# Experts packed by rank in grains of 32 rows, and weights held back until the first gather has landed

## The chip, the cores and the metric

The kernel runs on one core of one Trainium2 chip, in float32 throughout, as one launch. The metric is device time in microseconds (us); the median of three runs before is 3216.39 us.

## What is computed

A trunk of two layers over 1024 image tokens and 256 context tokens of width 1024. A layer is adaptive modulation, attention (differential attention over all tokens in layer 1, windowed attention with sinks in layer 2), a residual, and a hierarchical mixture of experts. Layer 1 sends 1280 tokens through the experts, layer 2 only the 1024 image tokens. The part that matters here, with `h` the normed tokens:

```python
grp    = argmax(softmax(h @ w_r1 + b_r1))              # one of 4 groups
p_in   = softmax((h @ w_r2 + b_r2)[grp])               # 8 experts of the group
top_p, top_j = top_k(p_in, 2);  top_p /= sum(top_p)
expert = grp * 8 + top_j                               # 2 of 32 experts a token
y      = (silu(g) * u) @ w2[expert],  g, u = split(h @ w13[expert])
out    = sum over the two experts of p_grp * top_p * y
```

`w13` of an expert is 1024 x 1024 and `w2` is 512 x 1024 (4 MiB and 2 MiB). Which rows belong to which expert is known only at run time.

## The kernel before

Every layer has five stages with a barrier of all engines between them (`phase_end`): front (modulation, QKV), attention, post (output projection, residual, norm, router logits), route (tables of where each row goes), and the experts. After layer 2 a last stage adds the weighted expert outputs. In the text, layer 1 is `l = 0` and layer 2 is `l = 1`.

*Post* (lines 1220 to 1357). One step for each tile of 128 tokens: PE makes the output projection (L1265), DVE takes it (L1307, L1308), DVE scales it (L1317), POOL shifts it (L1356), PE turns it (L1246), ACT and DVE copy it (L1334, L1288), PE makes the logits of the tile before (L1254) and DVE adds their bias (L1293).

*Route* (`dve_route`, L1401). DVE picks for all tiles together the group and the two experts of each token as one-hot rows, counts rows of each expert before each tile (L1439), PE adds them up over the partitions (L1553 to L1555), and DVE works out how many blocks of 128 and halves of 64 rows each expert needs. It writes `exptab`, the expert of each block, which SP reads to load weights (L1467), then for each row a block and a lane; 16 or 20 small pairs of one-hot maps (L1511, L1512) go through PE (L1559) and give `toktab` and `rowtab`, the token that is gathered for each lane of each block and the row that is scattered to (L1517 to L1521).

*Experts* (L1631 to L1942). The work is a fixed list of units of 128 rows. A unit is either one expert's block ("B") or two halves of 64 rows for two experts ("P"), by the strings `ORDER`: 27 units in layer 1, 23 in layer 2, 35 blocks or halves of each layer with 3 weight pieces of 2 MiB each: two for `w13`, one for `w2`. Pieces go one after another through a ring of nine slots: SP waits until the piece nine before has been used (L1615) and issues a transfer (L1616). The first nine are issued in the route stage as soon as `exptab` is there (L1634), before the barrier. POOL clears the gather buffers (L1642), loads a few constants in layer 1 (L1646), and gathers the tokens of a unit by an indirect DMA (L1655) up to two units ahead; it scatters a unit's output (L1662). PE does for unit i: gate/up (L1707, 16 products of 128 x 128 by 512, or 32 with 64 columns, whose two halves write to different PSUM partitions), turning the tokens of unit i+1 (L1691), down of unit i-1 (L1728), turning h of unit i (L1739). In the trace each float32 product is two records, one a pass. ACT and DVE copy in between. Rows that find no room go to fallback blocks (L1863 to L1942): a loop that runs at least once, each trip loading three pieces (L1857, L1859) and working one block of 128 rows with nothing overlapped.

## Time and profile before

| what | before |
|---|---|
| median of 3 runs | 3216.39 us (3216.09 to 3216.54) |
| profiled execution, its own time | 3216.31 us |
| its span, first to last instruction | 3214.7 us |
| PE busy | 2896.9 us (90%) |
| DVE, ACT, POOL busy | 40%, 25%, 21% |
| mean granted TensorE clock | 0.951 |
| read from and written to memory | 662.32 MB, 87.62 MB |
| first expert stage, first to last unit | about 1223 to 1827 us |
| second expert stage, first to last unit | about 2594 to 3122 us |

The span is the profiled execution from its first to its last instruction; times in the rows are microseconds from its start. A busy share is the part of a stretch in which the engine had an instruction; idle time counts only where the engine is what the end waits for. The granted clock is a share of 2.4 GHz.

### The profile page before, as it was taken

Reading aid. Unit: us, or ns where it says so; the run is one execution under the profiler, and the core shown is the slowest. Engines: PE = TensorE matmul, PEld = TensorE weight load, DVE = VectorE, ACT = ScalarE, POOL = GpSimd, SP = SyncE. Lnnn points to the kernel's source line nnn. Section 1 sums busy time; section 2 is a strip of 40 time slices with the busy share of each in tenths; the row PEclk is TensorE's granted clock in tenths of the full one; section 3 lists DMA queues with packets and bytes.
Section 4 is the critical chain, followed back from the end, with each engine's and each line's share of the span. In section 5 each row is a group of like instructions: output and inputs, shape, how many; then the busy total and the mean of one; then the engine's idle time right before and its main releaser. Section 6 shows DMA issues by size and latency. Waiting matters only on the chain. (4 is left out here: it accounts for less than half of the span.)

```text
span 3214.7 us, 34383 instructions
## 1 busy us (share of the span) xinstructions
PE 2896.9 (90%) x13041; PEld 1615.1 (50%) x13041; DVE 1299.6 (40%) x2274; ACT 792.7 (25%) x1763; POOL 689.5 (21%) x931
## 2 busy tenths in 40 slices
PE   7999998999999947999999959979999579999993
PEld 3444335888884533444444424468875334443431
DVE  4544204898882252111111154469972521111114
ACT  2211102777771100000000043146641000000001
POOL 2555201555452110010000024510001110000001
PEclk9999999999999958999999979989999789999996
DMA  6334576242413248999999574343322399999995
GB/s 252 100 102 138 199 267 176 52 98 50 99 54 128 92 188 332 412 386 415 383 413 389 216 270 135 88 124 56 67 67 93 130 410 427 426 427 427 426 417 208
DMA packets 205154, 734.36 MB, mean 228 GB/s; under 512 B 29376, under 2 KB 124784, under 8 KB 168896
## 3 DMA queue, kind: packets, MB, share of 16 engines
q1 hardware_dynamic: 104800, 633.33, 52.7%
q10 hardware_dynamic: 84896, 61.07, 5.8%
q0 software_dynamic: 15296, 37.78, 3.0%
q8 instruction: 104, 1.70, 0.2%
q14 instruction: 58, 0.48, 0.1%
HBM read 662.32 MB, written 87.62 MB: 233 GB/s over the span
## 5 line engine op out<-in xcount | busy, mean ns | idle before, releaser
L1707 PE MATMUL psum<-moe_ring,moe_xT 128*64 128x512 f32 (+1 forms) x2240 | 707.9, 602 | 15.6 <-DMA moe_ring<-in_e_w 13.3
L407 PE MATMUL psum<-qkv_w,act_hT 128*128 128x512 f32 x1376 | 612.0, 598 | 1.4 <-ACT act_hT L508 1.3
L1707 PEld LDWEIGHTS psum<-moe_ring,moe_xT 128*64 128x64 f32 (+1 forms) x2240 | 277.3, 162 | 410.4 <-issue 408.4
L407 PEld LDWEIGHTS psum<-qkv_w,act_hT 128*128 128x128 f32 x1376 | 256.6, 192 | 309.2 <-issue 306.9
L1728 PE MATMUL psum<-moe_ring,moe_hT 128*64 128x512 f32 (+1 forms) x1120 | 352.8, 594 | 1.6 <-DVE moe_hT L1808 1.6
L1804 DVE TENSOR_TENSOR moe_hh<-psum,moe_sg 128x512 f32<-128x512 f32 x50 | 34.6, 692 | 668.4 <-PE psum L1707 668.4
L1265 PE MATMUL psum<-wo,out_oT 128*128 128x512 f32 x576 | 255.6, 599 | 1.4 <-DVEq L1281 1.0
L1728 PEld LDWEIGHTS psum<-moe_ring,moe_hT 128*64 128x64 f32 (+1 forms) x1120 | 133.1, 160 | 184.6 <-issue 180.4
L1013 DVE TENSOR_REDUCE att_nmax<-psum 128x1 f32<-128x1280 f32 (+1 forms) x160 | 204.2, 1276 | 29.0 <-PE psum L906 28.0
L906 PE MATMUL psum<-att_kT,att_q 128*128 128x512 f32 (+1 forms) x832 | 198.0, 370 | 10.0 <-ACTq L137 5.1
L969 ACT ACTIVATE att_prob<-psum,att_nmax 128x1280 f32<-128x1280 f32 (+1 forms) x160 | 185.3, 1158 | 56.4 <-DVE att_nmax L1013 53.0
L1655 POOL DMA_INDIRECT moe_xg<-h_d,toktab x52 | 52.9, 1018 | 681.9 <-PE psum L1691 674.4
L1772 ACT ACTIVATE moe_sg<-psum 128x512 f32<-128x512 f32 x50 | 29.9, 598 | 670.9 <-PE psum L1707 670.9
L887 POOL TENSOR_SCALAR att_epsum<-att_den 128x1 f32<-128x1 f32 x80 | 112.7, 1408 | 325.9 <-DVE att_coef L1019 325.9
L954 PE MATMUL psum<-act_V,att_aT 128*128 128x128 f32 x1344 | 167.9, 279 | 4.1 <-DVE att_aT L1040 4.1
L1265 PEld LDWEIGHTS psum<-wo,out_oT 128*128 128x128 f32 x576 | 107.9, 192 | 126.7 <-issue 124.8
L906 PEld LDWEIGHTS psum<-att_kT,att_q 128*128 128x128 f32 x832 | 146.2, 191 | 38.2 <-ACT att_prob L969 6.1
L954 PEld LDWEIGHTS psum<-act_V,att_aT 128*128 128x128 f32 x1344 | 156.2, 192 | 9.8 <-DVE att_aT L1040 7.7
L605 POOL TENSOR_TENSOR qkv_t<-qkv_xn,qkv_rope 128x128 f32<-128x128 f32 (+1 forms) x264 | 133.0, 534 | 53.5 <-DVE qkv_xn L715 53.5
L1662 POOL DMA_INDIRECT y_d<-moe_yo,rowtab x50 | 50.3, 1005 | 395.3 <-ACT moe_yo L1778 395.3
L1068 PE MATMUL psum<-att_k,att_q 128*128 128x256 f32 x704 | 124.7, 305 | 6.9 <-ACTq L137 4.7
L911 PE MATMUL psum<-cst,att_prob 128*128 128x128 f32 x672 | 99.7, 277 | 18.8 <-DVE att_prob L1022 10.9
(252 smaller groups left out, 3301.7 us busy)
## 6 DMA issues: line engine op xcount, KB each, us to landing
moe_ring<-in_e_w SPq DMA_DIRECT2D x216, 2048.0 KB, 16.2
ada_w<-in_ada_w SPq DMA_DIRECT2D x48, 1024.0 KB, 6.5
qk_d<-qkv_stg ACTq DMA_DIRECT2D x112, 256.0 KB, 2.8
att_q<-qk_d SPq DMA_DIRECT2D x32, 640.0 KB, 12.5
att_q<-qk_d SPq DMA_DIRECT2D x64, 256.0 KB, 5.1
qkv_w<-in_a_wqkv SPq DMA_DIRECT2D x6, 2048.0 KB, 9.4
att_kT<-qk_d SPq DMA_DIRECT2D x32, 320.0 KB, 5.7
prep_y<-y_d SPq DMA_DIRECT2D x10, 1024.0 KB, 7.3
```

Of the source, the lines that this page charges most:

```text
L407: ins = nc.tensor.matmul(psum[:, u.par, :], hT[:, k, u.t * P:(u.t + 1) * P], qw[:, u.C % 2, k], start=(k == 0), stop=(k == KD - 1))
L605: ins = nc.gpsimd.tensor_tensor(dst[:, :, a, b, :], src[:, :, a, 1 - b, :], sn, ALU.mult)
L887: ins = nc.gpsimd.tensor_scalar(epsum[:, q], den[:, q, 0:1], den[:, q, 0:1], EPS, ALU.mult, ALU.mult)
L906: ins = nc.tensor.matmul(psum[:, 3 * m + b, 0:hi - lo], aq0[buf][:, m, x, t * P:(t + 1) * P], kT[buf][:, m, lo:hi], start=x == 0, stop=x == 1)
L911: ins = nc.tensor.transpose(psum[:, bank, (b - lo) * P:(b - lo + 1) * P], prob0[:, 2 * (n % 2), b * P:(b + 1) * P], ident)
L954: ins = nc.tensor.matmul(psum[:, 7, 0:P], aT0[:, n % 2, b, :], v, start=(b == 0), stop=(b == nb - 1))
L969: nc.scalar.activation(prob0[:, 2 * (n % 2) + m, 0:width], psum[:, 3 * m:3 * m + 3, :].rearrange("p b n -> p (b n)")[:, 0:width], ACT.Exp, ...
L1013: nc.vector.reduce_max(nmax[:, n % 2, m:m + 1], psum[:, 3 * m:3 * m + 3, :].rearrange("p b n -> p (b n)")[:, 0:width], AX, negate=True).th ...
L1068: ins = nc.tensor.matmul(o, aq1[:, half, m, j % 4, x, :], k, start=x == 0, stop=x == 1 and masked is None)
L1265: ins = nc.tensor.matmul(psum[:, 2 * par + n, :], oT[:, k, t * P:(t + 1) * P], wo[:, k, n * HALF:(n + 1) * HALF], start=(k == 0), stop=(k ...
L1707: ins = nc.tensor.matmul(psum[part, bank, :], xT[:, 4 * half + k, part], ring[:, w13[x, half] % RING, k, bank * DE:(bank + 1) * DE], start ...
L1728: ins = nc.tensor.matmul(psum[part, 5 + h, :], hT2[:, k, part], ring[:, w2[x] % RING, k, h * HALF:(h + 1) * HALF], start=(k == 0), stop=(k ...
```

## The change

The blocks and halves are replaced by grains of 32 rows. The 32 experts are ranked by their number of rows at run time, and each rank has a fixed room in grains (`ROOM`). The ranks are laid one after another, in the order that the string `STREAM` gives by room sizes, so that an expert may begin or end within a unit and a piece may serve two or more units. One rank of room 4 is left out of the units and takes the first fallback block (`own`), so 31 experts or 93 pieces stream through the ring. Within a unit all products have the same width: the largest of 1, 2 or 4 grains that divides each start and size (`columns`).

```diff
-ORDER = [("BBPBBPB" * 4)[1:], ("BP" * 12)[1:]]
+ROOM = [[5] * 3 + [4] * 5 + [3] * 12 + [2] * 11 + [1], [8, 8, 6, 5, 4] + [3] * 5 + [2] * 10 + [1] * 12]
+STREAM = ["4323532243235322432353224323312", "1218121822315213321312263122111"]
+GRAIN = 32
...
+        def columns(i):
+            width = max(n for n in (1, 2, 4) if all(at % n == 0 and size % n == 0 for r, at, size in UNITS[l][i]))
+            for r, at, size in UNITS[l][i]:
+                for b in range(at, at + size, width):
+                    yield r, slice(GRAIN * b, GRAIN * (b + width))
...
-                        for x in range(parts):
-                            part = slice(x * rows, (x + 1) * rows)
-                            ins = nc.tensor.matmul(psum[part, bank, :], xT[:, 4 * half + k, part], ring[:, w13[x, half] % RING, k, bank * DE:(bank + 1) * DE],
+                        for r, part in columns(i):
+                            ins = nc.tensor.matmul(psum[part, bank, :], xT[:, 4 * half + k, part], ring[:, CHUNK[l][r, half] % RING, k, bank * DE:(bank + 1) * DE],
```

A unit has one, two or four products of each kind side by side. A ring slot is given back when the last unit that uses its piece is done with it (`FREED`), and `s_used` counts half steps instead of pieces.

The first four pieces are issued in the route stage; the others wait until the first gather of tokens has landed:

```diff
+    HEAD = 4
...
     def sp_moe_first(sp, l):
         sp.wait_ge(s_exptab, l + 1)
-        sp_moe_loads(sp, l, 0, RING)
+        sp_moe_loads(sp, l, 0, HEAD)
 
     def sp_moe(sp, l):
-        sp_moe_loads(sp, l, RING, 10 ** 6)
+        sp.wait_ge(s_xg[0], xg_count(l, 0))
+        sp_moe_loads(sp, l, HEAD, 10 ** 6)
         sp_fallback(sp, l)
```

The picks are made tile by tile in the post stage, after the logits of the tile before (`dve_pick`, 19 DVE operations a tile, most of them chained):

```diff
+        def first_of(val, width, code, top, one):
+            low = lowfirst[:, NE - width:NE]
+            L(V_.reduce_max(top, val, AX))
+            L(V_.scalar_tensor_tensor(code, val, top, low, ALU.is_equal, ALU.mult))
+            L(V_.reduce_max(tops[:, 3:4], code, AX))
+            L(V_.tensor_scalar(one, code, tops[:, 3:4], None, ALU.is_equal))
...
             if later:
                 logit(t - 1, 1 - par)
+                dve.wait_ge(s_rld, 2 + T)
+                dvec.link(dve, dve_pick(dve, l, t - 1))
```

The route stage starts from the picks. It ranks the experts by count with a few small DVE steps and four small products on PE, writes `exptab` by rank, adds each rank's first row and room on PE, and makes the lane and block maps in two large operations for each of the two choices, in bf16, with the row number split over two sets of columns; 16 or 20 bf16 products of 154 columns replace the float32 ones of 80. POOL clears the gather buffers and loads the constants in the route stage (`pool_route`) instead of at the start of the experts:

```diff
+        V_.scalar_tensor_tensor(key[:, :], psum[:, 1, 0:NE], float(NE), iota[:, 0:NE], ALU.mult, ALU.subtract)
+        L(V_.scalar_tensor_tensor(keycol[small], psum[small, 3, 0:1], float(NE), col(0)[small], ALU.mult, ALU.subtract))
+        V_.tensor_scalar(ahead[small, 0], key[small], keycol[small], None, ALU.is_lt).then_inc(s_rtp, 1)
...
+        L(V_.tensor_copy(exptab[:, 0:NE], psum[:, 5, 0:NE]))
+        dve.sem_inc(s_exptab, 1)
...
+        for q in range(2):
+            V_.tensor_tensor(value[:, q, 0:nt, 1], onblk[:, q, 0:nt], cst[:, C_TOK:C_TOK + nt].unsqueeze(2).broadcast_to([P, nt, NBT]), ALU.mult)
+            V_.tensor_tensor(onlane[:, q, 0:nt], iota.unsqueeze(1).broadcast_to([P, nt, P]),
+                             lane[:, q, 0:nt].unsqueeze(2).broadcast_to([P, nt, P]), ALU.is_equal).then_inc(s_rtp, 1)
```

The shares of the two experts (`dve_shares`) are worked out at the start of the expert stage. The fallback loop runs once for `own` and once more for each block of rows beyond the rooms, and its gate/up waits for the two pieces of `w13` alone; `w2` has a semaphore of its own (`s_ow2`).

## Rows read from the trace of the kernel before

**Rows 1.** Stretches: us, busy time of each engine (records), PE clock, DMA share, GB/s.
```profile
1223.00:1827.00 604.00, 602.35 (x2004) 267.18 (x2004) 84.24 (x120) 48.78 (x82) 52.53 (x52) 0.99 0.94 380
2594.00:2858.00 264.00, 263.25 (x994) 110.51 (x996) 41.06 (x59) 21.61 (x36) 23.21 (x23) 0.99 1.00 421
2858.00:3104.00 246.00, 235.09 (x872) 98.69 (x871) 28.35 (x41) 17.93 (x30) 20.21 (x20) 0.98 1.01 427
```

**Rows 2.** Waits of PE from 2590 to 3170: us in total, times, longest.
```profile
PE psum L1707 <- DMA moe_ring<-in_e_w: 13.3, 6, 4.5
```

**Rows 3.** The chain that ended last: start us, us, what.
```profile
2580.38 11.09 DMA moe_xg<-h_d,toktab
...
3105.72 31.33 DMA moe_ring<-in_e_w
```

**Rows 4.** Timeline of PE in layer 1's experts: start us, us, what, records.
```profile
1242.32 13.95 PE L1707 MATMUL psum<-moe_ring,moe_xT 128*64 128x512 f32 x64
...
1264.54 13.90 PE L1707 MATMUL psum<-moe_ring,moe_xT 128*128 128x512 f32 x32
...
1286.86 13.47 PE L1707 MATMUL psum<-moe_ring,moe_xT 128*128 128x512 f32 x31
```

**Rows 5.** Timeline and durations (ns min/median/max) of the conditioning products, four side by side.
```profile
32.12 1.04 PE L374 MATMUL psum<-ada_w,ada_cs 128*2 128x512 f32 x8
...
L374 PEld LDWEIGHTS psum<-ada_w,ada_cs x384: 81/85/87, 11.6 to 523.6; 128*2 128x2 f32 x192
L374 PE MATMUL psum<-ada_w,ada_cs x384: 589/592/1061, 11.6 to 524.0; 128*2 128x512 f32 x192
...
L1707 PEld LDWEIGHTS psum<-moe_ring,moe_xT x2240: 132/137/337, 1223.6 to 3114.2; 128*64 128x64 f32 x100, 128*128 128x128 f32 x87
```

**Rows 6.** Timeline of DVE at the end of the post stages.
```profile
1137.22 1.23 DVE L1307 TENSOR_TENSOR postb_x<-psum,post_bc 128x1024 f32<-128x1024 f32 x1 [6.81 <-PE psum L1265]
...
1145.15 0.20 DVE L1293 TENSOR_TENSOR logits<-psum,brt 128x36 f32<-128x36 f32 x1 [1.92 <-PE psum L1254]
1147.71 0.69 DVE L1288 COPY postc_h2T<-psum 128x512 f32<-128x512 f32 x1 [2.37 <-PE psum L1246]
...
2535.45 0.20 DVE L1293 TENSOR_TENSOR logits<-psum,brt 128x36 f32<-128x36 f32 x1 [3.74 <-PE psum L1254]
```

**Rows 7.** Timeline of DVE and PE in layer 2's route stage.
```profile
2538.80 0.42 DVE L1410 TENSOR_TENSOR route_re<-route_re,route_ru 128x256 f32<-128x256 f32 x1
...
2545.65 1.54 DVE L1439 TENSOR_TENSOR route_pre<-route_pre,route_re 128x32 f32<-128x32 f32 x7
...
2551.93 0.95 DVE L1464 TENSOR_TENSOR route_cmp<-route_cum,cst 128x768 f32<-128x768 f32 x1
...
2554.27 0.18 DVE L1467 TENSOR_SCALAR exptab<-route_ebf 128x35 int32<-128x35 f32 x1
...
2569.24 7.12 PE L1559 MATMUL psum<-route_blk,route_lane 128*128 128x80 f32 x32 [19.19 <-DVEq L1514]
...
2577.41 0.20 DVE L1521 TENSOR_SCALAR toktab<-rowtab 128x80 int32<-128x80 int32 x1
```

**Rows 8.** Timeline of the start of layer 1's experts.
```profile
1209.28 1.14 POOL L1655 DMA_INDIRECT moe_xg<-h_d,toktab  x1 [5.96 <-DMA moe_xg<-in_consts]
...
1220.83 1.94 PE L1691 MATMUL psum<-cst,moe_xg 128*128 128x128 f32 x8 [21.81 <-DMA moe_xg<-h_d,toktab]
...
1223.68 2.05 PE L1707 MATMUL psum<-moe_ring,moe_xT 128*128 128x512 f32 x2 [0.91 <-issue]
```

**Rows 9.** Time to landing: the ring's first piece alone, then the two fallback gathers.
```profile
DMA to landing us min/median/max: 7.2/7.2/7.2
...
DMA to landing us min/median/max: 2.2/4.2/6.2
```

**Rows 10.** Queue of gathers and scatters (packets, MB, share); DMA over layer 2's experts (GB/s last).
```profile
q0 software_dynamic: 15296, 37.78, 3.0%
...
2611.00:3122.00 511.00, 497.36 (x1850) 209.81 (x1850) 61.66 (x90) 39.44 (x66) 42.43 (x42) 0.99 1.01 425
```

More of the change, by code:

```diff
@@ new lines, in build @@
+    mine = A("mine", [P, 2, TA, NE])
+    slot = A("slot", [P, 2, TA])
+    sloti = A("sloti", [P, 2, 2, TA], I32)
+    blkf = A("blkf", [P, 2, TA])
+    lane = A("lane", [P, 2, TA])
+    onlane = A("onlane", [P, 2, TA, P], BF16)
+    onblk = A("onblk", [P, 2, TA, NBT], BF16)
+    value = A("value", [P, 2, TA, 2, NBT], BF16)
+    table = A("table", [P, 2, NBT])
+    assert A.at <= M.at, (A.at, M.at)
+    key = R("key", [P, NE])
+    keycol = R("keycol", [P, 1])
+    ahead = R("ahead", [P, 2, NE])
@@ new lines, in pe_route @@
+        pe.wait_ge(s_rtp, 6 * l + 1)
+        nc.tensor.matmul(psum[small, 3, 0:2], tot[:, :], ones[:, 0:2], start=True, stop=True)
+        nc.tensor.matmul(psum[:, 1, 0:NE], ones[:, :], tot[:, :], start=True, stop=True).then_inc(s_rtm, 1)
+        nc.tensor.matmul(rank, tri, both[:, 0:nt], start=True, stop=False)
+        nc.tensor.matmul(rank, ones[:, :], pre[:, 0:nt], start=False, stop=False)
+        pe.wait_ge(s_rtp, 6 * l + 2)
+        nc.tensor.matmul(psum[:, 4, 0:NE], ones[small, :], ahead[small, 0], start=True, stop=True).then_inc(s_rtm, 1)
@@ L1603, in build @@
-    PLAN = chunk_plan()
+            for i in range(NU[l] + 1):
+                new = []
+                parts = {"half0": (i, 0), "up": (i, 1), "down": (i - 1, 2)}
+                for what, (n, piece) in parts.items():
+                    if not 0 <= n < NU[l]:
+                        continue
+                    for r, at, size in UNITS[l][n]:
+                        if (r, piece) not in chunk[l]:
+                            chunk[l][r, piece] = count
+                            new.append((count, r, piece))
+                            count += 1
+                        done[chunk[l][r, piece]] = (l, n, what)
+                    steps[1] += 1
+                    ready[l, n, what] = steps[1]
+                plan.append((l, i, new))
@@ L1605, in sp_moe_loads @@
+        return plan, chunk, ready, {n: ready[at] for n, at in done.items()}, count
+    PLAN, CHUNK, READY, FREED, _ = chunk_plan()
+    CHUNKS = [3 * (NE - 1) * (l + 1) for l in range(2)]
+    assert _ == CHUNKS[1]
     def sp_moe_loads(sp, l, first, last):
@@ L1742, in pe_moe @@
         turn_x(0)
[L1743 to L1745 removed]
+        for i in range(nu + 1):
             if i < nu:
[L1747 removed]
+                gate_up(i)
                 turn_x(i + 1)
             if i:
[L1750 removed]
+                down(i - 1)
             if i < nu:
@@ L1755, in used_by @@
     def used_by(l, i, what):
-        for pl, pi, w13, w2 in PLAN:
-            if pl == l and pi == (i if what == "up" else i + 1):
-                return 1 + max((w13 if what == "up" else w2).values())
+        return READY[l, i, what]
     def act_moe(act, l):
-        nu, base, xbase = len(UNITS[l]), UBASE[l], UBASE[l] + l
+        nu, base, xbase = NU[l], UBASE[l], UBASE[l] + l
         def take_x(i):
@@ L1840, in fallback_slot @@
     def fallback_slot(l, part):
-        return (sum(3 * (NBIG[n] + NSMALL[n]) for n in range(l + 1)) + part) % RING
+        return (CHUNKS[l] + part) % RING
     def sp_fallback(sp, l):
@@ L1846, in sp_fallback @@
         w2v = e_w2[l].rearrange("e (p k) f -> p e k f", p=P)
-        last = sum(3 * (NBIG[n] + NSMALL[n]) for n in range(l + 1)) + 2
         sp.wait_ge(s_fbtab, l + 1)
-        sp.wait_ge(s_used, last - RING + 1)
+        sp.wait_ge(s_used, max(FREED[CHUNKS[l] + part - RING] for part in range(3)))
         if l == 0:
@@ L1949, in build @@
     fu = A("u", [P, TX, D])
-    fxb = nc.alloc_sbuf_tensor_at("last_xb", [P, 5, D], F32, offset=arena0_at + 6 * 4 * D * 4)
+    SPARE = next(n for n in range(4, RING - 1) if not {n, n + 1} & {fallback_slot(1, part) for part in range(3)})
+    fxb = nc.alloc_sbuf_tensor_at("last_xb", [P, 5, D], F32, offset=arena0_at + SPARE * 4 * D * 4)
     def last_x(t):
```

486 lines of the change are left out of this document (236 added, 250 removed).

## The prediction, made blind

> **What bounds the kernel now.** I read four views in this order: busy time by stretch, PE's waits, one product of the expert stage followed in time, and the DMA's rate over the same stretch. The stretches show two expert stages of different kinds. In the first, from 1223 to 1827 us, PE is busy 602.35 of 604 us at a clock of 0.99, while the DMA engines have share 0.94 [rows 1]: PE alone is the bound. In the second the DMA share is 1.00 from 2594 and 1.01 from 2858 on, and PE falls to 235.09 busy of 246 us [rows 1]: there the weight stream is the bound. The waits agree: between 2590 and 3170 PE waits 13.3 us for weights, in six waits [rows 2]. At the end of that stage the chain waits 31.33 us, from 3105.72 to 3137.05, for the fallback block's weights [rows 3]. So a unit less is worth a whole unit in layer 1 (the first), and only its bytes in layer 2.
>
> **A unit in layer 1.** One unit is gate/up, turning the next tokens, down, and turning h. The unit with one expert starts at 1264.54 and the next at 1286.86: 22.32 us; the unit with two 64-row halves starts at 1242.32: 22.22 us [rows 4]. Two halves cost no more than one whole, since 64 records in 13.95 us stand against 32 in 13.90. I take 22.35 us. By the tables in the diff, layer 1 goes from 27 units to 23 and layer 2 from 23 to 19. In layer 1 that removes 4 x 22.35 = 89 us.
>
> **Is a set of four 32-column products as cheap as one?** By the plan 12 units of layer 1 and 11 of layer 2 run in width 32, with four products side by side. "Even widths" means that all products of a unit have its smallest common width. The nearest rows are the conditioning products, four at once with 2 columns each: 8 records (4 products, 2 passes) last 1.04 us, and one record alone 0.592 [rows 5]: with passes 0.434 us apart (13.90 us / 32 records [rows 4]) one product by itself would last 1.03. Their weight loads take 85 ns against 137 ns for 64 columns [rows 5], so 32 columns should take about 109 ns by the straight line. Four loads in a row are 0.44 us, just the length of a pass. Bounds of the extra cost of a four-part unit: below, 0 (a gain is excluded, since 512 columns stream either way); above, every load stands bare in front of its pass, 48 passes x 0.43 = 20.6 us. I take 0.15 us, because the two-part unit already shows loads of several tiles beside running passes for 0.05 us, and the four-way set of 2 columns shows it for four tiles. In sum 2 us in layer 1.
>
> The Trainium skill speaks against this: "TensorE: Matmul & The Clock Gate", section "Part 3: Packing small matmuls — row/col tiling", gives 3.07x for four tiles and 2.38x for three tiles of 32 columns, not 4x and 3x, and says that weight loads overlap running products only where the row group differs, which it doesn't here. By that a set costs 1.3 of one. Here the trace has two column tiles at 1.99x (13.95 against 13.90 us), which doesn't agree, and nothing with four full loads; the result that the rule gives is the second rival.
>
> **Fallback blocks.** I evaluated the reference's router on the reference's own inputs. Layer 1's experts need, in grains of 32 and by rank, 5 three times, 4 five times, 3 twelve times, 2 eleven times, 1 once: exactly the room given (94). Layer 2 needs 8, 8, 6, 5, then 3 six times, 2 ten times, 1 twelve times: all inside the room of 78. So no row overflows. Both kernels run one fallback block a layer; after, it holds the expert of rank 7 (rank 4 in layer 2). Its time, 24 us, is not changed. It waits for two of its three pieces instead of three.
>
> **Picks moved into the post stage.** 19 small DVE operations a tile. Seven linked ones take 1.54 us [rows 7], so 0.22 us each and 4.2 us a tile. They run between the logits of a tile and the next attention output, where DVE sits idle 6.81 us [rows 6]. So for all tiles but the last two they cost nothing; without that cover they'd cost up to 16 x 4.2 = 67 us. In the tail they are bare: the pick of the last but one tile starts at 1145.35 and ends near 1149.6, and pushes the copy at 1147.71 [rows 6] by 1.9 us; then come the last logits and a pick of 4.3 us. The same in layer 2: logits done 2535.65, now 2537.5, pick done 2541.9, barrier 2542.2.
>
> **Route stage, layer 2.** PE makes totals and ranks (3 us), then a ping-pong of small steps of 0.2 to 0.4 us with DVE for ranks of experts: the expert table is written some 4.2 us behind the barrier, at 2546.4, against 2554.45 now [rows 7]; the first weights go out 0.9 us later. PE's sums end at about 2548. Then DVE: 12 small steps 2.7, seven of 256 elements at about 0.4, 2.9, four small 0.8, two block maps of 616 elements 1.5, two values of 616 and two lane maps of 1024, 3.8 in all (0.95 us for 768 elements [rows 7]), 2559.8. 16 bf16 products follow, of which 8 lie behind the last map: 1.6 us against 7.12 now [rows 7]. Six steps for the table end at 2563, against 2577.6 now. Clearing the gather buffers (1.8 us) moves ahead, beside DVE's work. The gather goes out near 2563.9 instead of 2580.38 [rows 3]: 16.5 us earlier. In layer 1 the same steps with ten tiles give 1183.1 instead of 1209.28 [rows 8], 26 us earlier, since there the load of constants, now also ahead, had waited behind the ring's flood (about 6 us). Bounds of the new chain, some 50 dependent steps: 4 us either way a layer.
>
> **Weights held back.** The first gather takes 11.09 us beside nine queued pieces [rows 3] and 2.2 to 6.2 us at the fallback, beside few [rows 9]. With four pieces, started 17 us before, at 7.2 us for the first [rows 9] and 4.9 for each other, only one is still moving. I take 6. It lands at 2569.9 (now 2591.5) and 1189.1 (now 1220.8); the first product follows 2.9 us later [rows 8]: 1192.0 against 1223.68, so 31.7 us earlier in layer 1. The price is borne by SP: pieces 5 to 93 are queued behind its wait. The stream stands idle some 3 us in each layer, and in layer 2, whose first unit has three experts, piece 6 is late by about 5 us.
>
> **Sum, layer 1.** PE needs 23 x 22.35 = 514 us. The stream needs 93 pieces x 4.91 (2 MiB at 427 GB/s [rows 1]) = 457 us plus the rows moved by gathers and scatters: 37.78 MB in both layers [rows 10], five ninths of it here, 49 to 60 us. Both are nearly equal, and the stream has a head start of 28 us. I walked the plan unit by unit: a piece lands 4.91 us after the one before, but not before its slot (the piece nine before) was given back plus 2.3 us; each gather and scatter adds 1.05 to 1.5 us; PE waits where a piece is late. On the plan of before the walk gives 1828.0 for the start of the fallback against 1827, and 3137.3 against 3137.05 in layer 2. On the new plan PE waits 6.5 to 10.5 us, where units need four pieces in a row. Gain: 31.7 + 89.4 - 8 - 2 = 111 us.
>
> **Sum, layer 2.** The stream is the bound: 12 pieces fewer, 12 x 4.91 = 59 us; rows are as many as before. It runs at 425 GB/s [rows 10]. From 2572.2 on 89 pieces take 437 us, the rows some 46: 3055 at the least. An expert of eight grains keeps its three pieces through two units, and ring slots are given back in order, so the walk ends with the last piece at 3062 to 3069; the fallback's first two pieces follow 9.8 us later: it starts at 3072 to 3079 (3077 taken) against 3137.05. Gain 60 us: 59 for bytes, 8 for the earlier start, 5 for the third piece not waited for, less about 12 for slots and the hold. PE's waits rise there to over 70 us; that costs nothing while the stream is the bound. Everything else moves up unchanged.
>
> Profiled time 3216.31 (span 3214.7; the median of the runs is 3216.39) less 171: 3045 us.
>
> **The rivals.**
> 1. *Rows overflow the rooms.* My counts are in full precision; layer 1 has an expert with exactly 64 rows in a room of 64. One row too many costs one fallback trip: 24 us for the block and about 17 for its three pieces (2.3 + 3 x 4.91), 41 us: 3086. Against it: only ties could do it. 5%.
> 2. *Four tiles cost 1.3 of one.* 20.6 x 0.3 = 6.2 us a unit: 12 units, 74 us in layer 1. In layer 2, 71 us on 425 of PE work stay near the stream's 483; about 20 show. 3140. 9%.
> 3. *Weight loads of four tiles stand bare.* Twice the time for a set, 20.6 us a unit. Layer 1 loses 247 us against 111 of gain; layer 2's PE work, 425 + 11 x 20.6 = 652 from 2573, ends at 3225, about 90 later than before. 3216 + 136 + 90 = 3440, slower. It decides from about 10.6 us a unit (a set at 1.5 of one), where 12 x 10.6 plus what passes the stream in layer 2 eats 171. For it: the eight loads of a set sum to its whole length; against it, [rows 5]. 4%.
> 4. *The hold starves the ring.* If the gather lands as slowly as now (11 us), both layers start 5 us later and the early waits double: 3062. 10%, inside the range.
>
> **How the numbers follow.** The forecast has 72%; its own range is 3030 to 3066 (route 4 us a layer, rows' share 7, slots and clock after longer waits 6). The range 3026 to 3092 takes in rivals 1 and 4 and leaves out rivals 2 and 3, and some 6% of the unforeseen. A difference of 0.2% is 6.4 us, about what a measurement tells from none. Faster: all but rival 3 and a little: 0.95; same 0.01; slower 0.04.
>
> **What would show it.** Gate/up with 128 records in 13.9 to 14.1 us: right; 18 or more: rivals 2 or 3. Layer 1's first product near 1192 and the fallback at 1716. DMA share near 1.0 in layer 2 and PE waiting there for weights over 50 us. One fallback block a layer, 32 records each; more is rival 1. The pause of DVE before the next output shrinks from 6.8 to 2.6 us, with PE's pace in the post stage unchanged.

## The result, and the profile after

| | before | after |
|---|---|---|
| median of four runs on the same chip | 3216.24 us | 3063.16 us (3059.18 to 3066.86) |
| ratio, 95% interval | | 0.9524 (0.9508 to 0.9541) |
| profiled execution, its span | 3216.31, 3214.7 us | 3065.03, 3063.2 us |
| PE busy | 2896.9 us | 2743.3 us |
| moved by the DMA engines | 734.36 MB | 684.33 MB |
| mean granted clock | 0.951 | 0.950 |

The kernel is 4.8% faster. The forecast was 3045 us with a range of 3026 to 3092. The profiled execution is 20 us above its forecast: of the 171 us of gain, 151 came. Of the 20, 14.5 lie in layer 2's expert stage and 6.6 in layer 1's; the starts of both came a little earlier than forecast.

The span is best cut at four points: first product of layer 1's experts, first product of its fallback block, and the same two in layer 2.

| stretch | before | after | change | forecast |
|---|---|---|---|---|
| start to layer 1's experts | 1223.7 | 1191.3 | -32.4 | -31.7 |
| layer 1's experts | 603.5 | 530.8 | -72.7 | -79.3 |
| from there to layer 2's experts | 767.2 | 744.4 | -22.8 | -21.6 |
| layer 2's experts | 542.6 | 518.7 | -23.9 | -38.4 |
| fallback of layer 2 to the end | 77.6 | 78.0 | +0.4 | 0 |
| sum | 3214.7 | 3063.2 | -151.5 | -171 |

The first view is busy time by stretch, of the kernel after; its columns are those of [rows 1]. The first line is layer 1's experts, then four pieces of layer 2's experts, then that stage as a whole.

```profile
1191.00:1722.00 531.00, 521.37 (x3252) 200.34 (x3252) 68.83 (x103) 41.32 (x70) 44.46 (x44) 0.99 0.96 402
2466.00:2600.00 134.00, 122.42 (x596) 51.08 (x597) 18.42 (x30) 9.08 (x15) 10.07 (x10) 0.94 0.94 393
2600.00:2720.00 120.00, 111.57 (x629) 43.69 (x628) 13.84 (x20) 8.96 (x15) 10.11 (x10) 0.97 0.93 386
2720.00:2860.00 140.00, 114.36 (x832) 38.30 (x836) 12.77 (x19) 8.36 (x14) 9.10 (x9) 0.89 0.98 409
2860.00:2985.00 125.00, 104.97 (x820) 35.52 (x808) 12.82 (x19) 8.36 (x14) 9.39 (x11) 0.97 0.98 406
2466.50:2985.20 518.70, 453.29 (x2868) 168.53 (x2868) 57.38 (x85) 34.26 (x58) 38.52 (x40) 0.94 0.96 399
```

Read the last two numbers of each line. In layer 2 the DMA engines had a share of 1.00 to 1.01 and 421 to 427 GB/s before [rows 1]; now they have 0.96 and 399, and none of the four pieces reaches 1.00. PE is busy only 453 of 519 us. So neither PE nor the DMA engines are full: each waits for the other in turn. The waits show both sides. First PE's in the two expert stages (line of the waiting product, what it waited for, us in all, times, longest). Before, there were 13.3 us in six in layer 2 [rows 2] and none for weights in layer 1. The lines stand in the order layer 1, layer 2.

```profile
PE psum L1760 <- DMA moe_ring<-in_e_w: 8.2, 4, 3.2
...
PE psum L1760 <- DMA moe_ring<-in_e_w: 42.7, 12, 6.7
PE psum L1775 <- DMA moe_ring<-in_e_w: 16.3, 6, 5.2
PE psum L1935 <- DMA moe_ring<-in_e_w: 6.1, 1, 6.1
```

Then the waits of SP for a free ring slot from 2590 to 2990, in the same columns. SP issues the transfers, and it waits for PE to give back slots:

```profile
SPq L1683 <- PE psum L1760: 202.2, 17, 31.4
SPq L1683 <- PE psum L1775: 123.3, 8, 34.5
```

Before, in the same stage, its waits were short: the longest lasted 12.2 us, and there were 62 of them in 412 us.

```profile
SPq L1616 <- PE psum L1707: 268.5, 42, 12.2
SPq L1616 <- PE psum L1728: 143.9, 20, 7.4
```

Now 25 waits take 325 us, up to 34.5 us each: slots come back in bursts. SP waiting is harmless while enough transfers are still moving; where a wait outlasts them, the DMA engines run dry. The part on the prediction shows where that happens.

### The profile page after: what moved, and what is told of

Its sections match the earlier page's. It is cut to its first block, busy times and chain, and to the rows that moved or that the text cites. A ratio compares the mean times of both kernels' runs of the same rounds, so it can differ in the third digit from the quotient of the medians.

```text
span 3063.2 us, 38668 instructions
## 1 busy us (share of the span) xinstructions
PE 2743.3 (90%) x15193; PEld 1491.9 (49%) x15193; DVE 1299.9 (42%) x2420; ACT 781.0 (25%) x1743; POOL 673.5 (22%) x915
## 2 busy tenths in 40 slices
DMA packets 199412, 684.33 MB, mean 223 GB/s; under 512 B 26688, under 2 KB 122096, under 8 KB 166208
## 4 chain that ended last, share of the span: by engine, by line
PE 74%; DMA 13%; DVE 7%; issue 2%; ACT 1%; POOL 1%; SPq 1%; POOLq 0%; ACTq 0%; DVEq 0%
PE psum L443 17%; PE psum L1760 14%; DMA moe_ring<-in_e_w 11%; PE psum L1318 8%; PE psum L1775 8%; PE psum L990 4%; PE psum L942 4%; PE psum L1117 3%; PE psum L1104 2%; PE psum L947 2%; PE psum L1145 2%; PE psum L410 1%; PE psum L1737 1%; PE psum L1307 1%; PE psum L1935 1%
## 5 line engine op out<-in xcount | busy, mean ns | idle before, releaser
L1760 PE MATMUL psum<-moe_ring,moe_xT 128*32 128x512 f32 (+2 forms) x3744 | 610.9, 617 | 53.2 <-DMA moe_ring<-in_e_w 51.0
L1760 PEld LDWEIGHTS psum<-moe_ring,moe_xT 128*32 128x32 f32 (+2 forms) x3744 | 206.0, 124 | 427.0 <-issue 424.1
L1775 PE MATMUL psum<-moe_ring,moe_hT 128*32 128x512 f32 (+2 forms) x1872 | 301.5, 605 | 17.1 <-DMA moe_ring<-in_e_w 16.3
L1775 PEld LDWEIGHTS psum<-moe_ring,moe_hT 128*32 128x32 f32 (+2 forms) x1872 | 98.9, 122 | 188.1 <-issue 184.3
L1702 POOL DMA_INDIRECT moe_xg<-h_d,toktab x44 | 44.8, 1019 | 642.2 <-PE psum L1737 601.8
L1708 POOL DMA_INDIRECT y_d<-moe_yo,rowtab x42 | 42.2, 1005 | 376.5 <-ACT moe_yo L1818 376.5
L567 ACT ACTIVATE qkv_sq<-psum 128x512 f32<-128x512 f32 (+1 forms) x66 | 37.5, 568 | 318.3 <-PE psum L443 318.3
## 6 DMA issues: line engine op xcount, KB each, us to landing
att_q<-qk_d SPq DMA_DIRECT2D x32, 640.0 KB, 12.2
```

Source lines behind the costliest of these rows:

```text
L1760: ins = nc.tensor.matmul(psum[part, bank, :], xT[:, 4 * half + k, part], ring[:, CHUNK[l][r, half] % RING, k, bank * DE:(bank + 1) * DE], ...
L1775: ins = nc.tensor.matmul(psum[part, 5 + h, :], hT2[:, k, part], ring[:, CHUNK[l][r, 2] % RING, k, h * HALF:(h + 1) * HALF], start=(k == 0) ...
```

## The experiments

All were run beside the kernel before on the same chip; ratios are to that kernel, with 95% intervals. Where a kernel is compared with the kernel after, it is by medians, with 3063.16 us; the experiments used several chips, and the median of the kernel before differs by up to 0.7 us between them. Stage times are from one profiled execution of each. Layer 1's stage takes 530.8, 533.0 and 533.2 us in three kernels that are alike up to there, so a stage's difference of 2 or 3 us says nothing.

**Without the hold.** All nine first pieces are issued in the route stage, and SP waits for no gather.

```diff
-    HEAD = 4
+    HEAD = RING
...
-        sp.wait_ge(s_xg[0], xg_count(l, 0))
```

> The changed kernel with all nine pieces issued in the route stage and no wait for the first gather (HEAD = RING). Theory A (the hold only moves a few us about): the first gather lands some 4 us later in each layer (11 us beside nine pieces, 7.0 as changed); in layer 1 all of that shows, in layer 2 the stream gains some 8 us of idle time and loses the 4: in sum 0 to +5 us, 3063 to 3068. Rival (the hold starves the ring in layer 2 and is what the forecast missed): 10 to 15 us faster, 3048 to 3053.

Measured: 3065.93 us (3060.85 to 3069.25), ratio 0.9529 (0.9513 to 0.9545). In the profile both expert stages start later, layer 1's at 1199.6 and layer 2's 6.3 us later after layer 1's end; but layer 2's own stage is 508.8 us instead of 518.7. So the hold gains 8.3 and 6.3 us at the two starts and loses 9.9 in layer 2's stage; the net, 2.8 us by the medians, is within their spread. Theory A's range holds, and the rival's 10 to 15 us did not come.

**Six pieces ahead instead of four.** `HEAD = 6`, the wait for the gather kept.

> The changed kernel with six pieces issued before the hold instead of four, as layer 2's first unit needs six. Theory A (the stream's idle time at the start of layer 2 is late at its end): the waits of 1.8 and 1.9 us in layer 2's first unit go, the stream starts some 8 us further on, the first gather lands 1 to 2 us later in both layers: 4 to 8 us faster, 3055 to 3059. Rival (as with nine pieces, what the stream gains is given back later by slots that aren't free): within 3 us of 3063.

Measured: 3067.18 us (3063.06 to 3069.03), ratio 0.9537 (0.9521 to 0.9553). It lies at neither expectation: the 4 to 8 us of gain did not come, and it is 4.0 us above the kernel after, within the spread. The chain of waits (start, us, what) shows why the number of pieces ahead matters to the gather. In order: the gathers of the kernel after in layers 1 and 2, then those with six pieces, then those without the hold.

```profile
1183.14 5.13 DMA moe_xg<-h_d,toktab
...
2456.49 7.01 DMA moe_xg<-h_d,toktab
```

```profile
1183.85 11.37 DMA moe_xg<-h_d,toktab
...
2460.76 10.83 DMA moe_xg<-h_d,toktab
```

```profile
1184.90 11.72 DMA moe_xg<-h_d,toktab
...
2466.14 11.12 DMA moe_xg<-h_d,toktab
```

With two more pieces issued ahead of it the gather takes 11.37 and 10.83 us instead of 5.13 and 7.01; three more on top of them add next to nothing (11.72 and 11.12). Before, with nine, it took 11.09 us [rows 3].

**The hold alone, on the kernel before.** Blocks, halves, picks and route as before.

```diff
-        sp_moe_loads(sp, l, 0, RING)
+        sp_moe_loads(sp, l, 0, 4)
...
-        sp_moe_loads(sp, l, RING, 10 ** 6)
+        sp.wait_ge(s_xg[0], xg_count(l, 0))
+        sp_moe_loads(sp, l, 4, 10 ** 6)
```

> The kernel before with one part of the change alone: four pieces in the route stage, the others after the first gather has landed. Theory A (the hold helps the layer that PE bounds and costs the layer that the stream bounds): in layer 1 the constants' load and the gather no longer stand beside the ring, the first product comes 10 to 13 us earlier and so does the end of the stage; in layer 2 the first product comes 7 us earlier but the stream stands idle for 10 us, and the fallback starts 6 to 11 us later relative to the layer: in sum 0 to 6 us faster, 3210 to 3216. Rival (the hold is worth its gain in both layers): 15 to 20 us faster, 3197 to 3201.

Measured over ten runs: 3210.71 us against 3216.54, ratio 0.9981 (0.9972 to 0.9991), 5.8 us faster. Layer 2's gather lands after 3.48 us here. The profile shows 11.1 us gained at the start of layer 1's experts (1212.6 against 1223.7), 5.7 at the start of layer 2's, and 13.8 given back within layer 2's experts (556.4 against 542.6), where PE's waits rise from 13.3 to 26.0 us. Counted from the end of layer 1's experts, layer 2's fallback starts 8.1 us later (1317.9 against 1309.8 us). So also here layer 2 pays, as Theory A said.

**Products as wide as they can be.** A unit with 64 + 32 + 32 rows gets three products instead of four of width 32.

```diff
-            width = max(n for n in (1, 2, 4) if all(at % n == 0 and size % n == 0 for r, at, size in UNITS[l][i]))
             for r, at, size in UNITS[l][i]:
-                for b in range(at, at + size, width):
+                b = at
+                while b < at + size:
+                    width = max(n for n in (1, 2, 4) if b % n == 0 and b + n <= at + size)
                     yield r, slice(GRAIN * b, GRAIN * (b + width))
+                    b += width
```

> The changed kernel without even widths: an expert's grains in a unit are cut into the largest aligned products (3 grains are 64 + 32 columns), so that most four-part units become 64 + 32 + 32. Theory A (products of unequal width run side by side as well): gate/up stays at 13.9 us, the time within 4 us of 3063. Rival (the array takes only tiles of one width at once): a set costs two passes, 20 us more in each of 12 units of layer 1 and in about 6 of layer 2: about 3300 to 3400, slower than the kernel before.

Measured: 3493.45 us (3492.1 to 3494.86), ratio 1.0861 (1.0843 to 1.0879). Fewer products, 430 us more than the kernel after, and more than the rival's 3300 to 3400. The timeline of PE (start, us, what, records) shows two units of three products, and the first one's turning and down between them:

```profile
1210.52 31.80 PE L1762 MATMUL psum<-moe_ring,moe_xT 128*64 128x512 f32 x96
1242.25 1.16 PE L1737 MATMUL psum<-cst,moe_xg 128*128 128x128 f32 x8
1243.25 7.03 PE L1777 MATMUL psum<-moe_ring,moe_hT 128*128 128x512 f32 x16
...
1250.68 31.83 PE L1762 MATMUL psum<-moe_ring,moe_xT 128*32 128x512 f32 x96
```

96 records are 16 passes over `k` and bank, each a set of three products of two records: 31.80 / 16 = 1.99 us a set, against 0.87 us for a set of four of width 32 (13.94 / 16). Record by record, the product of 64 columns runs by itself for 1.00 us, and then the two of 32 run together for 0.98. Products of unequal width do not run side by side, in neither order: the first unit shown starts each set with the product of 64 columns, the second ends with it. By the tables, 12 units of layer 1 and 6 of layer 2 have such sets. In each, gate/up costs 17.9 us more and down 8.9 more (15.95 us against 7.07); the expectation had left out down. Layer 1's stage grew by 311 us and layer 2's by 119. The expectation's reason, that the array takes one width at a time, fits this, but only the times are shown.

**Width 32 in every unit.** `width = 1` in place of the `max`: the units of width 64 and 128 get four products too.

> The changed kernel with width 32 in every unit, also where one expert fills all four grains or two share it evenly: 64 products instead of 16 or 32. Theory A (four products of one width cost a set whatever they hold): within 4 us of 3063, though all units have four weight loads a pass. Rival (it is the number of products that made the unequal widths slow): some 7 + 6 whole units and 4 halves get slower by 10 us or more each, 3180 or more.

Measured: 3063.04 us (3062.18 to 3065.99), ratio 0.9524 (0.9509 to 0.954): no change. Two units in PE's timeline:

```profile
1232.55 13.94 PE L1760 MATMUL psum<-moe_ring,moe_xT 128*32 128x512 f32 x128
1246.42 1.16 PE L1737 MATMUL psum<-cst,moe_xg 128*128 128x128 f32 x8
1247.51 7.07 PE L1775 MATMUL psum<-moe_ring,moe_hT 128*32 128x512 f32 x64
1254.51 0.75 PE L1783 MATMUL psum<-cst,moe_hh 128*128 128x128 f32 x4
1255.19 13.94 PE L1760 MATMUL psum<-moe_ring,moe_xT 128*32 128x512 f32 x128
```

So it is the evenness that counts, not how many products there are, as Theory A said. Such a unit takes 22.64 us (1232.55 to 1255.19); the unit with two halves took 22.22 and the one with one expert 22.32 [rows 4].

**Half the bytes.** From the tenth piece of each layer on, only half of each piece is loaded; the products of the other half use old data, so the output is not the program's.

```diff
+                if n - CHUNKS[0] * l < RING:
...
+                else:
+                    src = w2v[:, ds(e, 1), 0:2, :] if piece == 2 else w13v[:, ds(e, 1), 4 * piece:4 * piece + 2, :]
+                    sp.dma_start(ring[:, n % RING, 0:2].rearrange("p k f -> p (k f)"), src.rearrange("p o k f -> p (o k f)")).then_inc(s_ring[n % RING], 16)
```

> The changed kernel with half of the bytes of every streamed piece left out from the tenth piece of each layer on (its products then use old data in the other half). It takes the weight stream away as a bound. Theory A (the stream bounds layer 2 and not layer 1): layer 1's experts get 8 to 10 us shorter (their waits), layer 2's some 70 to 80 (its 66 us of waits, and the slow halves behind them): about 2980. Rival (PE's own pace with four tiles, turns and copies has grown and bounds layer 2 too): 3030 or more.

Measured: 3062.94 us (3059.83 to 3065.15), ratio 0.952 (0.9504 to 0.9536). Theory A's 2980 did not come, and by the total it seems that the bytes cost nothing. The profile says otherwise. PE has no wait for weights in layer 1, and the stage takes 520.2 us instead of 530.8; layer 2's fallback starts at 2905.7 instead of 2985.2, 79.5 us sooner. What eats the gain is that the changed numbers of layer 1 route layer 2's tokens otherwise, so rows overflow and the fallback loop makes three trips instead of one. Its gate/up in PE's timeline, idle time before it in brackets:

```profile
2905.69 16.09 PE L1939 MATMUL psum<-moe_ring,moe_xT 128*128 128x512 f32 x32 [6.99 <-DMA moe_ring<-in_e_w]
...
2945.82 16.50 PE L1939 MATMUL psum<-moe_ring,moe_xT 128*128 128x512 f32 x32 [13.80 <-DMA moe_ring<-in_e_w]
```

A trip is 40.1 us, two of them 80. That is the price that the first rival put at 41. And the part on the stream is clear: with its bytes halved, PE's waits in layer 2 (the fallback's apart) fall from 59.0 to 11.0 us, and the stage from 518.7 to 450.4 (Theory A: layer 1's experts 8 to 10 us shorter, layer 2's 70 to 80).

**Idle products before the waits.** In layer 2 PE makes 33 products of constants that nothing reads, one to four before each of 16 waits, so that it is not idle there.

```diff
+        def fill(i, piece):
+            for n in range(FILL.get((i, piece), 0)):
+                nc.tensor.matmul(psum[:, 7, :], ident, cst[:, C_COS:C_COS + HALF], start=True, stop=True)
...
+                fill(i, half)
                 arrived(i, half)
```

> The changed kernel with idle products put on PE ahead of 16 of its waits for weights in layer 2 (one to four of 0.86 us each, into an unused bank), never longer than the wait they stand in. It keeps PE at work so that its clock does not fall: as changed, ten halves behind waits take 8.4 to 9.8 us instead of 7.07, 21 us in sum. Theory A (this is what the forecast missed: slow halves give their ring slots back late): 15 to 20 us faster, 3043 to 3048, and no slow halves. Rival (the stream bounds the stage whatever PE's clock is, and the slow halves lie in time that PE would have waited): 0 to 5 us faster, 3058 to 3063.

Measured: 3056.35 us (3052.38 to 3059.28), ratio 0.9498 (0.9483 to 0.9514), 6.8 us less than after; neither theory's number. The single times just touch (the slowest here is 3059.28, the fastest after 3059.18). What it meant to fill is seen in PE's timeline of the kernel after. All three lines are half a gate/up of width 32, of 64 records:

```profile
2692.39 9.72 PE L1760 MATMUL psum<-moe_ring,moe_xT 128*32 128x512 f32 x64 [4.28 <-DMA moe_ring<-in_e_w]
...
2710.47 7.07 PE L1760 MATMUL psum<-moe_ring,moe_xT 128*32 128x512 f32 x64
...
2815.17 9.77 PE L1760 MATMUL psum<-moe_ring,moe_xT 128*32 128x512 f32 x64 [6.72 <-DMA moe_ring<-in_e_w]
```

Ten pieces of work (eight halves of a gate/up and two downs), each behind a wait of 2.0 to 6.7 us, take 8.4 to 9.8 us instead of 7.07, 21 us more in sum. All seven that stand behind a wait of 4 us or more are among them, but one behind 3.03 us took 7.07. The granted clock of the stretch 2720 to 2860 is 0.89. With the idle products the clock of the stage rises from 0.94 to 0.98:

```profile
2470.00:2979.00 509.00, 468.75 (x2934) 178.34 (x2934) 57.41 (x86) 34.31 (x58) 37.40 (x39) 0.98 0.97 406
```

Layer 2's stage is 9.4 us shorter in the profile (509.3). Of the 21 us only 6.8 come out at the end. Where the stream sets the time, a slower PE only uses up a wait that it would have had anyway; it costs just where it gives back a slot too late. This reading fits both kernels that were filled, but no run tested it apart.

**Another order of the experts.** Same rooms, same units, same bytes; only the order in which ranks are laid changes, so that experts that need many pieces alternate with ones that need few.

```diff
-STREAM = ["4323532243235322432353224323312", "1218121822315213321312263122111"]
+STREAM = ["2333523223534223351423432433222", "1613113822228222513231321111211"]
```

> The changed kernel with the ranks laid in another order (the two strings of STREAM alone), found with the recurrence of the prediction after two of its terms were set to what the changed kernel shows (3.0 us from a freed slot to a transfer under way, 1.3 to 1.5 us for each gather and scatter). The new orders avoid units with three experts next to experts that go through two units. Theory A (late slots are what is left of the stream's idle time): layer 1 waits nowhere, -10 us; layer 2 ends 10 us earlier: 3043 to 3048. Rival (the order doesn't matter, the memory itself delivers 400 instead of 427 GB/s beside the gathers): -7 us at most from layer 1's waits, 3056 to 3060.

Measured: 3039.62 us (3038.75 to 3041.24), ratio 0.9451 (0.9435 to 0.9467), 23.5 us less than after. Layer 1's stage is 8.6 us shorter (522.2) and has no wait for weights; layer 2's is 14.6 shorter (504.1), and in its line of busy time by stretch the DMA's rate is up from 399 to 411 GB/s:

```profile
2457.80:2962.00 504.20, 450.16 (x2821) 165.83 (x2821) 57.35 (x86) 34.30 (x58) 36.64 (x37) 0.94 0.98 411
```

The clock of the stage stays at 0.94, so what the stages gain does not come from the clock. Another 3 us come behind them: the last block's gate/up takes 14.00 us instead of 17.02, and from there to the end it is 74.9 us instead of 78.0. The time is below Theory A's 3043 to 3048, and the rival (the order doesn't matter) is excluded.

**Order and head together.** A third order for layer 2, in which the first units need fewer pieces, with four pieces ahead in layer 1 and six in layer 2.

```diff
+STREAM = ["2333523223534223351423432433222", "1211122262331182211253231283111"]
...
+    HEAD = [4, 6]
```

> The order of e7_streams for layer 1, and for layer 2 one found in the same way with six pieces ahead of the hold; four pieces ahead in layer 1 and six in layer 2. Theory A (six pieces cost 3 us at the first gather of layer 2 and give 9 in the stream, and the start of layer 1 keeps its 7 us): 4 to 8 us faster than e7_streams, 3032 to 3036. Rival (the stream gives the gain back, as in e2_head6): 3037 to 3043.

Measured: 3036.53 us (3034.2 to 3038.62), ratio 0.9445 (0.9429 to 0.9461). It is the fastest version run, 26.6 us under the kernel after, and layer 2's stage is down to 498.9 us. The gain over the other order, 3.1 us, is less than the 4 to 8 of Theory A. The ratio intervals of this and the version ahead of it overlap, so the 3.1 us between them are likely, not shown.

**That version with idle products.** 31 of them before nine waits in layer 2, as above.

> e10_order_head46 with idle products on PE ahead of nine waits of layer 2 (31 products of 0.86 us in all, one less than fits each wait of the run before). Theory A (as in e5_fill, most of what the clock costs lies in waits anyway): the slow halves, 15 us in sum, go, the time falls by 4 to 8 us to 3029 to 3033. Rival (the stream sets the end, PE's clock doesn't matter): 3034 to 3038.

Measured: 3038.83 us (3036.9 to 3039.21), ratio 0.9446 (0.9433 to 0.9458): no gain, though the granted clock of the stage rises here as well:

```profile
2462.80:2960.80 498.00, 464.63 (x2594) 182.68 (x2594) 57.41 (x86) 34.30 (x58) 37.42 (x40) 0.98 0.98 411
```

The version without them has 0.94 and 410 GB/s there, in 498.9 us. In this kernel a higher clock in the stage buys nothing, as the rival said.

**The fallback waits for all its pieces again.** `s_ow2` is waited for ahead of gate/up, as before.

```diff
+            pe.wait_ge(s_ow2, 16 * B + 16)
...
-            pe.wait_ge(s_ow2, 16 * B + 16)
```

> The changed kernel with the fallback's gate/up waiting for all three pieces again (w2's wait stands ahead of it). Theory A: in layer 2 the fallback starts one piece later, +4.9 us, in layer 1 its pieces are there long before and nothing changes: 3068. Rival (the third piece is hidden by others anyway): 3063.

Measured: 3064.53 us (3062.42 to 3070.71), ratio 0.9524 (0.9508 to 0.954). In the profile the fallback's wait in layer 2 is 9.7 us instead of 6.1 and layer 2's stage 5.3 us longer, but that execution was the slowest of its four; the medians differ by 1.4 us, which is less than their spread. Between Theory A (4.9 us) and the rival (none) this decides nothing.

## Why the prediction was right, and what it mis-sized

**The bounds of the two stages.** Right. With half the bytes layer 1's stage shrinks by 10.6 us of 530.8 and layer 2's by 68.3 of 518.7: PE bounds the first, the stream with its holes the second.

**Four products of 32 columns.** Right: 13.94 us for 128 records, within the 13.9 to 14.1 named, against 13.90 for one product of 128 [rows 4]. Rivals 2 and 3 are excluded. The loads of 32 columns take 106 to 110 ns (shortest and median), as the straight line had it, and eight of them stay hidden in a set of 0.87 us. The profile's rows of both kinds of unit in layer 1:

```profile
1209.24 13.94 PE L1760 MATMUL psum<-moe_ring,moe_xT 128*32 128x512 f32 x128
...
1254.08 13.90 PE L1760 MATMUL psum<-moe_ring,moe_xT 128*128 128x512 f32 x32
1276.48 13.94 PE L1760 MATMUL psum<-moe_ring,moe_xT 128*32 128x512 f32 x128
```

The Trainium skill's 3.07x for four tiles ("TensorE: Matmul & The Clock Gate", section "Part 3: Packing small matmuls — row/col tiling"), which its table gives for tiles of 32 rows, is not what this trace shows for four of 32 columns: 3.99x (4 x 13.90 / 13.94) with 16 sets in a row. Another rule of the Trainium skill bears on the unequal widths: "TensorEngine Tiling (Array Packing)", section "Key Properties", says that changing the tiling mode drains the engine. The experiment agrees as far as widths in turn do not overlap; the rule gives no number for it, and here it is 1.99 us a set of three.

**The cost of a unit.** Here the term "0.15 us for a four-part unit, 2 us in sum" was too small. Setting aside the first and the last unit of the stage, which are special in both kernels, the 25 units between them took 22.17 us each before. After, the 21 between them span 481.9 us (1209.24 to 1691.17). Less 8.2 of waits and 1.7 for one slow half (1489.37, 8.77 us) that makes 22.48 us each, 0.31 more: 6.5 us in the layer. The rows of the all-32 kernel show where it lies: from the end of gate/up to the next one it takes 8.77 us (1246.42 to 1255.19), while before it took 8.33 (1788.20 to 1796.53), though down by itself is only 0.04 us longer in the rows. From start to start the turning before down takes 1.09 us instead of 0.99, down 7.00 instead of 6.87, and turning h 0.68 instead of 0.47. These are the joints between width 32 and width 128; that the change of width is the reason was not tested by itself. The same steps in PE's timeline of the kernel before:

```profile
1788.20 1.16 PE L1691 MATMUL psum<-cst,moe_xg 128*128 128x128 f32 x8
1789.19 7.03 PE L1728 MATMUL psum<-moe_ring,moe_hT 128*128 128x512 f32 x16
1796.06 0.63 PE L1739 MATMUL psum<-cst,moe_hh 128*128 128x128 f32 x4
1796.53 13.90 PE L1707 MATMUL psum<-moe_ring,moe_xT 128*128 128x512 f32 x32
```

**Layer 1's sum.** 603.5 - 4 x 22.17 + 8.2 + 1.7 + 6.5 makes 531.2 us against 530.8 measured. The waits were put at 6.5 to 10.5 us and are 8.2. That PE would wait there at all was foreseen, and all four waits are in units where two experts begin. The stage is 6.6 us longer than forecast: 4.5 for the unit's cost (6.5 instead of 2), 1.7 for the slow half; that a unit of before costs 22.17 and not 22.35 us makes 0.7 more, and the first unit is as much shorter. The shorter fallback wait does not reach here.

**The starts.** Right, to 1.2 us in both layers, in layer 2 with two errors that offset each other: counted from the end of layer 1's experts, the gather went out 18.7 us earlier (forecast 16.5) and took 7.01 us (forecast 6). The picks cost what was written: DVE's pause before the next attention output is down from 6.81 [rows 6] to 2.71 us (forecast 2.6), and PE's pace there is the same (16.39 us a tile). The gather went out at 1183.14 us (forecast 1183.1). Here are the pause, the gather, and the turning behind it, in the timeline after:

```profile
1105.43 1.23 DVE L1391 TENSOR_TENSOR postb_x<-psum,post_bc 128x1024 f32<-128x1024 f32 x1 [2.71 <-PE psum L1318]
...
1183.14 1.14 POOL L1702 DMA_INDIRECT moe_xg<-h_d,toktab  x1 [20.65 <-DVEq L173]
...
1188.41 1.95 PE L1737 MATMUL psum<-cst,moe_xg 128*128 128x128 f32 x8 [7.66 <-DMA moe_xg<-h_d,toktab]
```

Without the hold the two starts are 8.3 and 6.3 us later, so of the 32.4 and 22.8 us gained the picks and the route bring 24 and 16.5. In layer 1 the gather took 5.13 us.

**The price of the hold.** The prediction put it at some 3 us of idle stream and a late sixth piece. With six or nine pieces ahead layer 2's stage takes 508.2 and 508.8 us instead of 518.7, so by the stage alone the price is 10 us. Part of that is only that the hold lets the stage start earlier. From the first transfer issued (2440.3, 2444.6, 2450.0 us) to the fallback's first product (2985.2, 2982.8, 2989.0) the kernel after takes 544.9 us, with six pieces ahead 538.2, with nine 539.0: 6 to 7 us, in one profiled execution of each. At the hold itself the stream loses about 1.7 us: it moves 29, 246 and 279 GB/s in the three microseconds from 2464. The start gained makes up for the price in sum, so the total that rival 4 named (3062) is near, but not by its cause: the gather was not slow.

**Layer 2's stage.** This is the step that failed in size: "less about 12 for slots and the hold". With its start, layer 2 gained 46.7 us (22.8 + 23.9) where 60 were forecast; with the other terms as written, the 12 should have been 25. The first transfer went out 10 us earlier, not 8, counted from the end of layer 1's experts, so it is rather 27. The stage moved 399 GB/s for 518.7 us; at the 422 GB/s of before the same bytes take 518.7 x 399 / 422 = 490.4, so 28 us went as holes in the stream. Five stretches hold 26 of them (an estimate: the share by which each is below 422, times its length). The last two numbers are DMA share and GB/s:

```profile
2551.00:2563.00 12.00, 12.00 (x49) 5.78 (x42) 2.77 (x4) 1.79 (x3) 2.02 (x2) 1.00 0.31 82
2627.00:2635.00 8.00, 8.00 (x29) 3.67 (x31) 1.96 (x3) 0.83 (x2) 1.01 (x1) 1.00 0.37 125
2698.00:2705.00 7.00, 7.00 (x53) 3.02 (x46) 1.38 (x2) 1.20 (x2) 1.02 (x1) 1.00 0.56 194
2837.00:2845.00 8.00, 8.00 (x80) 2.47 (x76) 0.00 (x0) 0.00 (x0) 0.00 (x0) 1.00 0.58 202
2968.00:2973.00 5.00, 2.98 (x25) 1.14 (x16) 0.69 (x1) 0.60 (x1) 0.98 (x1) 1.00 0.50 167
```

Between them the rate is 412 to 426 GB/s, so the memory is not slower than before. PE is busy all through the first four: there it isn't PE that waits, and what PE lacks later are the pieces not sent then. In each of the first four SP stands at a slot of an expert that two units use. The first and largest: SP issues nothing from 2527.9 to 2560.7, since the next slot holds `w2` of an expert of eight grains, and the down product of its second unit ends at 2560.4. The second is the same with the other expert of eight grains (2606.3 to 2634.1). The third has two waits. SP issues two transfers at 2656.6 and 2657.1, of which the first lands 35.71 us later (chain of waits). It issues only one more at 2688.3 and the next at 2702.3, since both need slots of an expert of six grains that two units use.

```profile
2656.55 35.71 DMA moe_ring<-in_e_w
```

PE waits 4.28 us, until 2692.39, for that first transfer. Its granted clock, which has two levels of 1.2 and 2.4 GHz, falls from 1.00 (all at 2.4) to 0.62 over the next stretch, its half takes 9.72 us instead of 7.07, and the slot comes back 2.65 us later, in the hole:

```profile
2660.00:2690.00 30.00, 26.42 (x166) 10.41 (x164) 2.77 (x4) 1.79 (x3) 2.02 (x2) 1.00 1.01 427
2690.00:2694.00 4.00, 1.61 (x8) 0.45 (x12) 0.00 (x0) 0.00 (x0) 0.00 (x0) 0.62 0.99 423
2694.00:2705.00 11.00, 11.00 (x73) 4.14 (x66) 1.38 (x2) 1.20 (x2) 1.02 (x1) 0.83 0.73 280
```

With the orders of the faster version the stage takes 504.2 us at 411 GB/s, which leaves 13 us of holes (504.2 x 11 / 422). That is the same gain of 14.6 us read from the rate, not a second proof; what bears on the cause is that only the order was changed. That kernel still has two large holes, from about 2609 to 2621 and from 2699 to 2709. Without the hold the holes are still there (the first from about 2558 to 2570), and the stage's rate is 402: 24 us by the same sum. So the hold is a small part of them.

The walk through the plan had this mechanism (it says that an expert of eight grains keeps its three pieces through two units), but not its size. The expectation of the other order names what the author then put in to fit the kernel after, 3.0 us from a freed slot to a transfer under way instead of 2.3, and 1.3 to 1.5 us for each gather and scatter. That either is right by itself was not shown.

**Waits of PE.** "Over 70 us" in layer 2; it is 65.1, the fallback's included. "That costs nothing while the stream is the bound" is nearly so: filling the waits gained 6.8 us here and nothing in the faster version.

**Fallback.** One block a layer with 32 records, as evaluated. Rival 1 did not occur, and the half-byte kernel shows its price. The 5 us for the third piece not waited for are not settled: 1.4 by the medians, 5.3 by the profiled stage.

**A slip.** Rival 2's extra work in layer 2 is 11 x 6.2 = 68 us, not 71; nothing else changes by it.

**What stays open.** How much each cause of the 28 us of holes is worth by itself. Taken one at a time, another order shortens layer 2's stage by 14.6 us, idle products by 9.4, and two more pieces ahead by 10.5, of which 6 to 7 count from the first transfer. They do not add up: order and six pieces together shorten it by 19.8, and idle products on top of that by 0.9. The order changes both how long slots are kept and how many pieces a unit needs at once, and no run parts the two; none moved the turn-around of a slot.

## What to carry to other kernels

When a packing removes work from a stage where PE and a stream are nearly equal, count the stream's holes, not only its bytes: a ring of slots that come back in order runs dry when one user keeps its slot for two units, and the order of the users is then worth more (23.5 us here, for a changed string) than the clock or the number of products. Products of small, equal width side by side are nearly free (0.31 us of a unit of 22.2); unequal ones are not. A transfer that is held back for a small urgent one gains at the start and is paid for later by whatever is queued behind the wait, so try the number held for each stage by itself. And before a stage's time is read as a price, ask whether only its start has moved.

## What the runs showed of the hardware that was not expected

- Column products of unequal width do not overlap: a set of 64 + 32 + 32 columns takes 1.99 us, a set of four of 32 takes 0.87.
- A gather of 128 rows takes 5.1 and 7.0 us with four pieces of 2 MiB issued ahead of it, 11.4 and 10.8 with six, and 11.7 and 11.1 with nine: from six to nine there is hardly any rise.
- Behind each of seven waits of 4 us or more PE took 8.4 to 9.8 us for work that else takes 7.07, with a granted clock of 0.89 over such a stretch. Filling the waits restored the clock to 0.98 but moved the end by 6.8 us in one kernel and not at all in another.
